# Rows of a mixture-of-experts stage: one-hot products for every chunk, or one scatter to memory and two loads for each chunk

## The reference, cut to what matters

```python
def moe_ffn(h, w_router, b_router, w_up, b_up, w_down, b_down):
    xt = h.reshape(-1, D)                                   # D = 1024
    logits = (xt @ w_router + b_router)
    top_v, top_i = lax.top_k(logits, TOP_K)                 # 4 of 32
    wts = jax.nn.softmax(top_v, axis=-1)
    gate_dense = jnp.sum(jax.nn.one_hot(top_i, N_EXPERTS) * wts[..., None], axis=1)
    out = jnp.zeros_like(xt)
    for e in range(N_EXPERTS):
        z = xt @ w_up[e] + b_up[e]                          # 1024 -> 2048
        gate = jnp.minimum(z[:, :D_EXPERT], 7.0)
        up = jnp.clip(z[:, D_EXPERT:], -7.0, 7.0)
        act = (up + 1.0) * gate * jax.nn.sigmoid(1.702 * gate)
        out = out + gate_dense[:, e:e + 1] * (act @ w_down[e] + b_down[e])
    return out.reshape(B, T, D)
```

## Time and profile before

| | us |
|---|---|
| median of 3 runs | 1718.34 (1717.71 to 1719.27) |
| the profiled execution | 1717.43 |
| its span, first to last instruction | 1715.7 |
| PE busy in the span | 1498.3 (87%) |
| DVE, ACT, POOL busy | 379.5, 292.2, 84.0 |
| first chunk's up product begins | 676.1 |
| last chunk's down product ends | 1669.9 |

### The profile page before, as it was taken

One profiled execution on the slowest core, in us unless ns is written; L12 is line 12 of the kernel. 1 busy time (PEld: TensorE's weight loads), 2 busy tenths in 40 slices (PEclk: granted clock), 3 DMA queues, 4 the chain that ended last, 5 costly groups with the idle time before them and its releaser, 6 DMA issues.

```text
span 1715.7 us, 21858 instructions
## 1 busy us (share of the span) xinstructions
PE 1498.3 (87%) x8288; PEld 661.2 (39%) x8289; DVE 379.5 (22%) x804; ACT 292.2 (17%) x543; POOL 84.0 (5%) x122
## 2 busy tenths in 40 slices
PE   5989989779977955999999999999998998999980
PEld 4554445458854532333333232333332232332220
DVE  6110014256613243101011001011110010010106
ACT  5000006435321010111111101111111011011110
POOL 1000003200000000000000000000000000000002
PEclk9999999878987966999999999999999999999995
DMA  9774664961164623996999999899999999999954
GB/s 276 236 262 152 232 236 145 286 223 45 50 179 165 247 99 146 399 417 259 412 417 419 419 416 419 349 417 419 418 417 419 417 419 418 417 419 417 418 223 156
DMA packets 139315, 527.59 MB, mean 308 GB/s; under 512 B 11553, under 2 KB 40633, under 8 KB 104258
## 3 DMA queue, kind: packets, MB, share of 16 engines
q1 hardware_dynamic: 128482, 482.83, 71.9%
q0 software_dynamic: 10784, 44.07, 7.6%
HBM read 499.87 MB, written 31.15 MB: 310 GB/s over the span
## 4 chain that ended last, share of the span: by engine, by line
PE 55%; DMA 20%; SPq 11%; DVE 7%; issue 3%; ACT 2%; DVEq 0%; POOLq 0%; ACTq 0%; POOL 0%
PE bank L1278 19%; DMA arena<-in_b_up 14%; SPq L630 9%; PE bank L1300 6%; PE bank L1130 4%; PE bank L739 3%; DMA arena<-in_w_in 3%; PE bank L954 2%; PE bank L955 2%; SPq L635 2%; PE bank L1272 2%; PE bank L1203 2%; DMA arena<-in_cache_cmp,arena 1%; PE bank L1191 1%; DMA arena<-in_w_ada 1%
## 5 line engine op out<-in xcount | busy, mean ns | idle before, releaser
L1278 PE MATMUL bank<-arena 128*64 128x512 f32 x2176 | 494.1, 613 | 0.0
L1278 PEld LDWEIGHTS bank<-arena 128*64 128x64 f32 x2176 | 156.1, 140 | 338.6 <-issue 338.6
L1300 PE MATMUL bank<-arena 128*64 128x512 f32 x1088 | 254.9, 622 | 0.0
L2079 DVE TENSOR_SCALAR arena<-bank 128x512 f32<-128x512 f32 x34 | 23.5, 692 | 836.7 <-PE bank L1278 836.7
L1300 PEld LDWEIGHTS bank<-arena 128*64 128x64 f32 x1088 | 77.6, 142 | 153.8 <-issue 153.8
L1590 ACT ACTIVATE arena<-arena 128x512 f32<-128x512 f32 x34 | 21.5, 631 | 525.9 <-DVE arena L2079 525.9
L1248 PE MATMUL bank<-arena 128*64 128x512 f32 (+1 forms) x420 | 103.2, 609 | 8.0 <-DVE arena L2069 8.0
L2156 POOL DMA_DIRECT2D slots<-arena x68 | 36.0, 530 | 1299.0 <-ACT arena L1597 1296.8
L1130 PE MATMUL bank<-arena 128*128 128x288 f32 x256 | 78.7, 460 | 14.3 <-DMA arena<-in_w_in 11.1
L1272 PE MATMUL bank<-arena 1*64 1x512 f32 x272 | 40.3, 664 | 37.1 <-DMA arena<-in_b_up 35.5
L1130 PEld LDWEIGHTS bank<-arena 128*128 128x128 f32 x256 | 53.0, 216 | 31.9 <-DMA arena<-in_w_in 12.8
(11 more groups left out here) (392 smaller groups left out, 1304.9 us busy)
## 6 DMA issues: line engine op xcount, KB each, us to landing
arena<-in_w_up SPq DMA_DIRECT2D x256, 1024.0 KB, 19.2
arena<-in_w_down SPq DMA_DIRECT2D x128, 1024.0 KB, 22.6
arena<-in_w_ada SPq DMA_DIRECT2D x12, 2048.0 KB, 10.8
slots<-arena POOLq DMA_DIRECT2D x2, 6400.0 KB, 36.9
arena<-in_w_in SPq DMA_DIRECT2D x6, 2048.0 KB, 13.6
slots<-arena POOLq DMA_DIRECT2D x68, 128.0 KB, 5.5
arena<-in_w_in SPq DMA_DIRECT2D x16, 512.0 KB, 4.1
arena<-in_w_out SPq DMA_DIRECT2D x1, 4096.0 KB, 16.5
```

What stands on the lines that cost most here:

```text
L1278: last = mm(banks[part][SLOT * s:SLOT * s + SLOT, :], xcT[:, q], ring[pos][:, D * part + 512 * s:D * part + 512 * s + 512], start=False, s ...
L1300: last = mm(banks[4][SLOT * s:SLOT * s + SLOT, :], lhs, ring[pos][:, D * v + 512 * s:D * v + 512 * s + 512], start=False, stop=f == 7)
```

## The change

The buffer `slots` gets two more chunks of rows. As soon as the places are known, POOL scatters the normed rows to `slots` by 12 indirect transfers (one for each row block and choice). PE's one-hot product is made for chunk 0 only. For each later chunk ACT issues two transfers (64 rows x 512 columns each) that read its 64 rows from `slots` to `xr`; the loads of chunk c + 2 are issued in ACT's round c, behind the copy L1594. PE waits for them (`ld_xr`) where it waited for ACT's copy of bank 5. Since `slot_of` is needed for chunk 0 only, DVE's four operations become three over 12 elements per partition. ACT waits for the scatters (`scattered`) before the first load, which stands ahead of chunk 0's sigmoid. Results are written over the rows of their own chunk, as before.

```diff
--- before.py
+++ after.py
@@ -374,7 +374,7 @@
             dram[name] = nc.dram_tensor(name, shape, F32, kind="Internal").ap()
             return dram[name]
 
-        slots = internal("slots", (NCHUNK * SLOT, D))
+        slots = internal("slots", ((CMAX + 3) * SLOT, D))
         modd = internal("modd", (1 + NS, 4 * D))
 
 
@@ -474,11 +474,11 @@
         h2r = view(n_t, 3 * D, 3, D)
         h2T = mT
         gt, up, sg, ac = (view(gate_at + 512 * i, 512) for i in range(4))
-        in_chunk = [view(gate_at + 12 * NCHUNK * i, 12 * NCHUNK, 12, NCHUNK) for i in range(2)]
+        in_chunk = [view(gate_at + 12 * i, 12) for i in range(2)]
         aT, yc, xr = (view(x_at + 3 * D + 512 * i, 512) for i in range(3))
         xcT = view(mod_rows_at + 3 * D, 512, KD, SLOT)
         oneslot = view(mod_rows_at + 3 * D + 512, 3 * SLOT, 3, SLOT)
-        slot_of = view(mod_rows_at + 3 * D + 512 + 3 * SLOT, 3 * NCHUNK, 3, NCHUNK)
+        slot_of = view(mod_rows_at + 3 * D + 512 + 3 * SLOT, 3)
         bias = view(mod_rows_at, 2 * D)
         ring_at = fr["at"]
         assert ring_at + 16 * 2 * D <= arena_w and ring_at + 8 * 2 * D <= wo_at
@@ -1278,8 +1278,6 @@
                                     last = mm(banks[part][SLOT * s:SLOT * s + SLOT, :], xcT[:, q],
                                               ring[pos][:, D * part + 512 * s:D * part + 512 * s + 512], start=False, stop=q == 7)
                             last.then_inc(S("piece_used"), 1)
-                        pe.wait_ge(S("oneslot"), c + 2)
-                        dispatch()
                         pe.wait_ge(S("act"), c + 1)
                         for k in range(4):
                             last = nc.tensor.transpose(banks[3][:, P * k:P * k + P], ac[:, P * k:P * k + P], ident)
@@ -1287,7 +1285,7 @@
                         pe.wait_ge(S("yc"), c)
                         for s in range(2):
                             mm(banks[4][SLOT * s:SLOT * s + SLOT, :], one(s), row(s)[:, 512:1024], start=True, stop=False)
-                        pe.wait_ge(S("xr"), c + 2)
+                        pe.wait_ge(S("ld_xr"), c * 32 + 32)
                         chunk_T()
                         pe.wait_ge(S("aT"), c + 1)
                         for q in range(8, 12):
@@ -1585,17 +1583,26 @@
             nc.scalar.copy(xr, banks[5][:]).then_inc(S("xr"), 1)
             act.wait_ge(S("xcT_ps"), 1)
             nc.scalar.copy(xcT_half, by_half).then_inc(S("xcT"), 1)
+
+            def load_rows(c):
+                for s in range(2):
+                    act.dma_start(xr[SLOT * s:SLOT * s + SLOT], slots[bass.ds(c * SLOT, SLOT), 512 * s:512 * s + 512]
+                                  ).then_inc(S("ld_xr"), 16)
+
+            act.wait_ge(S("scattered"), 16 * 12)
+            for s in range(2):
+                act.dma_start(xr[SLOT * s:SLOT * s + SLOT], slots[SLOT:2 * SLOT, 512 * s:512 * s + 512]).then_inc(S("ld_xr"), 16)
             with act.Fori(0, n_chunks) as c:
                 act.wait_ge(S("gate"), c + 1)
                 fn(sg, gt, ACT.Sigmoid, scale=1.702).then_inc(S("sig"), 1)
-                act.wait_ge(S("xr_ps"), c + 2)
-                nc.scalar.copy(xr, banks[5][:]).then_inc(S("xr"), 1)
                 act.wait_ge(S("xcT_ps"), c + 2)
                 nc.scalar.copy(xcT_half, by_half).then_inc(S("xcT"), 1)
+                load_rows(c + 2)
                 act.wait_ge(S("piece_used"), c * 12 + 12)
                 act.wait_ge(S("st_yc"), c * 32)
                 nc.scalar.copy(yc, banks[4][:]).then_inc(S("yc"), 1)
             act.wait_ge(S("st_yc"), n_chunks * 32)
+            act.wait_ge(S("ld_xr"), n_chunks * 32 + 32)
             nc.scalar.copy(gathered, eps_t).then_inc(S("all_out"), 1)
             for i in range(3):
                 root_mean_square(i, 9 + i)
@@ -2059,22 +2066,15 @@
                                                             rowf[0:r, 4 * i + k:4 * i + k + 1]))
                 V.tensor_copy(rowu[0:r, 4 * i:4 * i + 4], rowf[0:r, 4 * i:4 * i + 4]).then_inc(S("rows"), 1)
 
-            link(dve, "dve", V.tensor_tensor(in_chunk[0], rowf.unsqueeze(2).broadcast_to([P, 12, NCHUNK]),
-                                             C("chunk0").unsqueeze(1).broadcast_to([P, 12, NCHUNK]), ALU.subtract))
+            link(dve, "dve", V.tensor_scalar(in_chunk[0], rowf, 1.0, None, ALU.add))
             link(dve, "dve", V.scalar_tensor_tensor(in_chunk[1], in_chunk[0], SLOT + 0.5, in_chunk[0], ALU.is_lt, ALU.mult))
-            link(dve, "dve", V.tensor_scalar(in_chunk[1], in_chunk[1], 0.0, None, ALU.max))
-            link(dve, "dve", V.tensor_reduce(slot_of, in_chunk[1].rearrange("p (i k) c -> p i c k", k=4), AX, ALU.add))
-
-            def one_slot(c):
-                V.tensor_tensor(oneslot, C("slot1").unsqueeze(1).broadcast_to([P, 3, SLOT]),
-                                slot_of[:, :, c].broadcast_to([P, 3, SLOT]), ALU.is_equal).then_inc(S("oneslot"), 1)
-
-            one_slot(slice(0, 1))
+            link(dve, "dve", V.tensor_reduce(slot_of, in_chunk[1].rearrange("p (i k) -> p i k", k=4), AX, ALU.add))
+            V.tensor_tensor(oneslot, C("slot1").unsqueeze(1).broadcast_to([P, 3, SLOT]),
+                            slot_of.unsqueeze(2).broadcast_to([P, 3, SLOT]), ALU.is_equal).then_inc(S("oneslot"), 1)
+
             after(dve, "tab")
             n_chunks = dve.value_load(tab[0:1, E - 1:E], min_val=E, max_val=CMAX)
             with dve.Fori(0, n_chunks) as c:
-                dve.wait_ge(S("xr_ps"), c + 1)
-                one_slot(bass.ds(c + 1, 1))
                 dve.wait_ge(S("piece_used"), c * 12 + 8)
                 V.tensor_scalar(gt, banks[0][:], 7.0, None, ALU.min).then_inc(S("gate"), 1)
                 V.tensor_scalar(up, banks[1][:], -7.0, 7.0, ALU.max, ALU.min).then_inc(S("up"), 1)
@@ -2146,7 +2146,13 @@
                                ).then_inc(S("zero_slots"), 16)
             pool.wait_ge(S("zero_slots"), 32)
 
+            pool.wait_ge(S("h2"), 3)
             pool.wait_ge(S("rows"), 3)
+            for i in range(3):
+                for k in range(4):
+                    pool.indirect_dma_start(
+                        out=slots, out_offset=bass.IndirectOffsetOnAxis(ap=rowu[0:ROWS[i], 4 * i + k:4 * i + k + 1], axis=0),
+                        in_=h2r[0:ROWS[i], i], in_offset=None).then_inc(S("scattered"), 16)
             after(pool, "tab")
             n_chunks = pool.value_load(tab[0:1, E - 1:E], min_val=E, max_val=CMAX)
             with pool.Fori(0, n_chunks) as c:
```

## The result

The changed kernel takes 1768.03 us (median; 1767.38 to 1770.24), the kernel before 1718.03 us in the same comparison: the ratio is 1.0294, 95% interval 1.0276 to 1.0312. It is 50 us slower; the prediction said 29 and its range ended at 1766. The profiled execution took 1767.86 us, with a span of 1766.1.

What follows compares the result with a forecast made beforehand. PE and transfers were taken to bound the kernel in turns. PE's way to chunk 14 +13.0, chunk 14 +2.5, loads of 18 chunks +11.3, last chunk +2.5: together +29.3 us, forecast 1747, range 1731 to 1766.

Steps and rivals of the forecast that it cites:

- the price of a row load: Each later chunk's 256 KB of rows, on the weights' engines, costs 0.63 us at 418 GB/s; bounds 0.4 and 1.26.
- the transfers' way to chunk 14: Up to chunk 14, transfers come 11.9 us later, ten loads included; PE's own way, 13.0 later, counts.
- the loads cost double: Rival: row loads cost twice their bytes, through 64 partitions and 2 KB rows; +45.9 us, 1764; chance 0.12.
- the equal share per MB of POOL's transfers: Evidence against double cost: POOL's small transfers held the engines 2.7% per MB, the weights 2.6%.
- The price of the hole: PE's new 3.09 us standstill between L1278 and L1285 lowers the clock, 2.5 us a chunk; bounds 0 and 3.4.
- the clock holds: Rival: PE's clock stays up through the hole in each chunk; +14.9 us, 1733; chance 0.17.
- The two edges and the alternation: PE sets the time in chunks 0 to 3, 14 and the last; transfers set it in between.
- The start: Before chunk 0, shorter DVE operations for the places end 2.7 us earlier, for PE too.
- The scatter: POOL's twelve indirect transfers land at 684 to 689, before chunk 0's sigmoid needs them; cost 0.
- the scatter lands late: Rival: the twelve scatters run one after another, hold chunk 0 by 50 us; 1797; chance 0.04.
- The loads in time: Row loads, needed some 25 us after issue, land in 5.5 us, 24.4 at most, before L1254; no wait.
- The rate of two hardware queues: Rival: ACT's queue beside SP's lifts the saturated rate above 418 GB/s; 1710 at an assumed +4.5%; chance 0.05.

Runs made afterwards that it cites:

- e3_one_load: The changed kernel with each chunk's 64 rows loaded by one transfer to 128 partitions instead of two to 64 each: 1749.06 us, ratio 1.0196.
- e6b_pool_loads: The changed kernel with its two loads to 64 partitions issued by POOL on its software queue instead of by ACT: 1766.80 us, ratio 1.0290.
- e9_half_load: The changed kernel with half of each chunk's rows left out, the other 128 KB loaded by one transfer to 64 partitions: 1749.83 us, ratio 1.0204.
- e5_two_full: The changed kernel with two loads a chunk, each to all 128 partitions and 256 of the 512 columns: 1750.59 us, ratio 1.0210.
- e2_fill_hole: The changed kernel with chunk 0's one-hot product made again in every round, unused, so PE has no hole: 1758.00 us, ratio 1.0255.
- e4_no_loads_fill: The changed kernel without the row loads in the loop and with the hole filled by an unused one-hot product: 1712.74 us, ratio 0.9995.
- e7_one_load_fill: The changed kernel with one load to 128 partitions a chunk and the hole filled by an unused one-hot product: 1731.75 us, ratio 1.0100.
- e10_half_full: The changed kernel with half of each chunk's rows left out, the other 128 KB loaded by one transfer to 128 partitions: 1747.05 us, ratio 1.0191.

## Why the prediction was wrong

**The step that failed is the price of a row load**, in the part on the row loads: 0.63 us, with 1.26 as the upper bound. It measured 1.53 us, above the upper bound too. In the 18 chunks from chunk 15 on that is 27.5 us for the 11.3 of the sum, 16 us of the miss, and it made the transfers' way to chunk 14 the longer one, 2 us more. That the loads take from the same capacity as the weights was right; that they take no more than their bytes was not. The rival "the loads cost double" was nearest, with 0.12 and a price still too low. Of its two reasons the rows of 2 KB fell (e3_one_load has them too, for 0.65 us), and the 64 partitions are what the runs point to. What was held against it, the equal share per MB of POOL's transfers, was the wrong row: those read SBUF and write memory. In every run that loaded 64 partitions the rate dipped at each load, from either queue, alone or in pairs (the changed kernel, e6b_pool_loads, e9_half_load); the same bytes to 128 partitions cost 0.65 us by one transfer and 0.71 by two (e3_one_load, e5_two_full). Why loads to 64 partitions do this no run shows, nor what part the pattern of reading has, which changed along with them.

**The price of the hole** was 2.5 us and measured 3.0 (bounds 0 and 3.4): on average 30.1 us a chunk instead of 29.6, about 6 us of the miss; the 1.3 us by which chunk 0 came out shorter than the sum had it (30.6 us instead of 31.9) are taken off already. (The terms come to 25 us: the 21 us between +29 and +50, and the 3.8 us that the profiled execution's mixer was quicker.) That the gated product, and with it `act`, would not come earlier, so that the removed 2.89 us leave a hole of 3.1 (it is 2.92) and gain nothing, is shown by the 2.92 us wait for L2086 in every chunk; that the hole acts through the clock by e2_fill_hole. The rival "the clock holds" fell.

The rows of before could have said so. The prediction read what a wait costs from L1272 and L1278 alone. One of its ten starts seemed to pay nothing (after 2.34 us of wait), but it paid later in the same chunk, with 8.58 us for L1300 instead of 7.09:

```profile
1610.75 13.97 PE L1278 MATMUL bank<-arena 128*64 128x512 f32 x64
...
1629.96 8.58 PE L1300 MATMUL bank<-arena 128*64 128x512 f32 x32
```

Counted over whole chunks (what L1272, L1278, L1254 and L1300 took beyond 1.09, 13.96, 0.66 and 7.09 us) all ten paid, 1.6 to 4.3 us and 2.8 on average, near the 3.0 that the hole cost.

**The two edges and the alternation** held: the ring was full at 780 to 800 (150 GB/s), PE set the time of chunks 0 to 3, 14 and the last. e4_no_loads_fill and e7_one_load_fill come out near what this account expected, 1712.74 and 1731.75 for 1715 and 1733, both counted from a kernel before at 1718.

**The start** held: from the end of the routing to the first one-hot product 5.9 us instead of 8.6, 2.7 less.

**The scatter** held at nothing. Its twelve transfers, and the load that waits for them:

```profile
659.76 1.01 POOL L2153 DMA_INDIRECT slots<-arena  x1 [325.39 <-DVE arena L2067]
...
673.43 0.85 POOL L2153 DMA_INDIRECT slots<-arena  x1 [0.31 <-issue]
...
679.09 1.21 ACTq L1594 DMA_DIRECT2D arena<-slots  x2
...
686.31 0.63 ACT L1597 ACTIVATE arena<-arena 128x512 f32<-128x512 f32 x1 [4.56 <-DVE arena L2079]
```

The last is issued at 674.3, ACT's wait ends by 679.1, and the sigmoid that stands behind it (L1597) runs at 686.3, as soon as DVE's L2079 is done. The rival "the scatter lands late" fell.

**The loads in time** held: they landed after 8.3 us at most, where 25 are there, and PE never waited for `ld_xr`.

**The rate of two hardware queues** did not rise: it is 406 GB/s in the changed kernel, and 417 in e3_one_load, which has two such queues too.

## What to carry to other kernels

Where transfers set the pace, price a new one by what it does to the rate of all the others, not by its bytes: load all 128 partitions at once rather than 64 and 64, and look for dips in the slices. Work on PE that seems hidden may be covering a wait for another engine; taking it out then gains nothing and leaves a hole that can cost more than the work did. When you read the price of a wait from a trace, follow it to the end of the stretch, since a drop of the clock can come later than the wait. Ask also which limit decides each stretch and how far behind the other one is: up to chunk 14 the two were 2 us apart, so that one repair alone gave little there and both together much.

## What the runs showed of the hardware

A load from memory of 128 KB to 64 partitions cost the saturated transfers about 0.74 us, of which its bytes are 0.31; to 128 partitions 0.38 us (e9_half_load, e10_half_full; the pattern of reading differs too). Stores from 64 partitions, 128 KB each, leave no dip of this kind: 418 GB/s beside them in the kernel before, 417 in e3_one_load.

A hole of 2.92 us in PE's work, behind 14 us of dense products and ahead of 2.2 us of transposes and one-row products, was followed by work at the lower of PE's two levels in every chunk that nothing else delayed, for 1.6 to 3.3 us of loss; six products of no use in the hole took the loss away there (e2_fill_hole, granted clock 1.00). In chunk 0 and after waits for a bias the lower level shows in the filled kernel too, and once in the kernel before it shows in a chunk without any wait (28.75 us from 788.45 to 817.20, instead of 27.10).
